# A three-block transformer on one core: the weight slots begin 64 bytes later in each partition

## The reference, cut to what matters

```python
x = layer_norm(x);  h = x @ w_in;  mix = mixer(h) @ w_out;  x = norm(alpha * x + mix)
ff = square(relu(x @ w1 + b1)) @ w2 + b2;                   x = norm(alpha * x + ff)
```

## Time and profile before

| | us |
|---|---|
| three runs | 3723.48, 3723.66, 3726.18 |
| median | 3723.66 |
| profiled execution, first to last instruction | 3724.2 |
| TensorE busy with matmuls | 3666.2 (98%) |
| VectorE busy | 2145.1 (58%) |
| ScalarE busy | 1580.6 (42%) |

### The profile page before, as it was taken

How to read it: one execution, slowest core, us unless ns; L and a number is a source line. 1 busy time by engine, 2 the same in 40 slices (tenths; PEclk the granted TensorE clock), 3 DMA queues, 4 the chain that set the end, 5 groups by cost and what they waited for, 6 DMA issues and landing times.

```text
span 3724.2 us, 50652 instructions
## 1 busy us (share of the span) xinstructions
PE 3666.2 (98%) x21121; PEld 2969.4 (80%) x21121; DVE 2145.1 (58%) x3262; ACT 1580.6 (42%) x2544; POOL 80.6 (2%) x85
## 2 busy tenths in 40 slices
PE   8999899999999999999999999999999999999998
PEld 5887778778888878888788889888787788788887
DVE  5641687775335578757587563366555266555333
ACT  5451566644334444435344452333343333434333
POOL 0000121000000000000000000000000000000000
PEclk9999899999999999999999999999999999999999
DMA  5124321324322222222222222222222222223232
GB/s 198 46 73 109 75 68 50 117 91 115 103 94 96 91 81 80 95 92 95 85 80 92 96 91 86 91 85 80 85 97 91 91 85 85 80 96 114 96 96 85
DMA packets 118490, 340.27 MB, mean 91 GB/s; under 512 B 20072, under 2 KB 31864, under 8 KB 118136
## 3 DMA queue, kind: packets, MB, share of 16 engines
q1 hardware_dynamic: 116024, 331.52, 27.3%
q0 software_dynamic: 2240, 5.51, 0.7%
HBM read 318.47 MB, written 20.06 MB: 91 GB/s over the span
## 4 chain that ended last, share of the span: by engine, by line
PE 95%; DVE 3%; ACT 1%; issue 1%; DMA 0%; SPq 0%; ACTq 0%; DVEq 0%
PE ps L329 54%; PE ps L307 28%; PE ps L1324 1%; PE ps L808 1%; PE ps L2833 1%; PE ps L1032 1%; PE ps L1647 1%; PE ps L1680 1%; PE ps L1335 1%; DVE n_s L1769 1%; PE ps L2262 0%; DVE g_D L1511 0%; PE ps L2289 0%; PE ps L1367 0%; PE ps L2251 0%
## 5 line engine op out<-in xcount | busy, mean ns | idle before, releaser
L329 PE MATMUL ps<-a,w_hi 128*128 128x512 f32 (+1 forms) x6064 | 1838.2, 388 | 2.5 <-ACT l_vf L2669 0.8
L329 PEld LDWEIGHTS ps<-a,w_hi 128*128 128x128 f32 x6064 | 1110.0, 188 | 259.5 <-issue 10.6
L329 PE MATMUL ps<-a,w_lo 128*128 128x512 f32 (+1 forms) x3032 | 1147.2, 385 | 0.0
L268 DVE TENSOR_TENSOR w_lo<-w_raw,w_hi 128x1024 fp32r<-128x1024 f32 x539 | 658.0, 1221 | 400.1 <-ACT w_hi L263 397.3
L263 ACT ACTIVATE w_hi<-w_raw 128x1024 fp32r<-128x1024 f32 x539 | 563.4, 1050 | 513.1 <-DMA w_raw<-in_w_mlp 324.1
L329 PEld LDWEIGHTS ps<-a,w_lo 128*128 128x128 f32 x3032 | 562.5, 188 | 120.0
L307 PE MATMUL ps<-h_hi,w_hi 128*128 128x512 f32 x1528 | 485.5, 399 | 0.0
L307 PE MATMUL ps<-h_lo,w_hi 128*128 128x512 f32 x1528 | 478.9, 395 | 0.0
L307 PE MATMUL ps<-h_hi,w_lo 128*128 128x512 f32 x1528 | 478.9, 395 | 0.0
L374 DVE TENSOR_TENSOR h_lo<-u_sq,h_hi 128x512 fp32r<-128x512 f32 x192 | 132.9, 692 | 460.7 <-ACT h_hi L364 459.8
L390 DVE TENSOR_TENSOR xT<-xT,ps 128x1024 f32<-128x1024 f32 x191 | 232.9, 1219 | 247.0 <-PE ps L307 246.0
(11 more groups left out here) (392 smaller groups left out, 2957.0 us busy)
## 6 DMA issues: line engine op xcount, KB each, us to landing
w_raw<-in_w_mlp SPq DMA_DIRECT2D x384, 512.0 KB, 3.4
w_raw<-in_w_in SPq DMA_DIRECT2D x107, 512.0 KB, 3.4
w_raw<-in_w_out SPq DMA_DIRECT2D x48, 512.0 KB, 3.4
n_bias<-na_tab SPq DMA_DIRECT2D x36, 256.0 KB, 4.7
xT<-in_x SPq DMA_DIRECT2D x8, 512.0 KB, 8.9
x<-xT SPq DMA_DIRECT2D x2, 2048.0 KB, 8.4
g_row<-gate_rows SPq DMA_DIRECT2D x16, 256.0 KB, 3.3
xT<-x SPq DMA_DIRECT2D x2, 2048.0 KB, 12.7
```

What stands on the lines that cost most here:

```text
L268: nc.vector.tensor_tensor(w_lo[u.z][:, :], w_raw[u.z][:, :], w_hi[u.z][:, :].bitcast(F32), ALU.subtract).then_inc(w_split[u.z], 1)
L329: last = nc.tensor.matmul(ps[:, bank, 0:t1 - t0], w[:, k * P:(k + 1) * P], a[:, h, low, k, t0:t1], start=(i_k == 0 and i == 0), stop=(i_k ...
```

## The change

A gap of 64 bytes is put ahead of the slots and one of 192 bytes behind them. So the slots move by 64 bytes, and everything behind them by 256. `slots_at` follows the slots.

```diff
         x_at = keep.at
         xT = keep.take("xT", [P, DC, T])
+        keep.at += 64
+        w_at = keep.at
         w_raw, w_lo, w_hi = [], [], []
         for z in range(SLOTS):
             w_lo.append(Region(keep.at, end).take(f"w_lo{z}", [P, UNIT], F32R))
             w_raw.append(keep.take(f"w_raw{z}", [P, UNIT]))
             w_hi.append(keep.take(f"w_hi{z}", [P, UNIT], F32R))
+        keep.at += 192
         params = keep.take("params", [P, NPARAM])
...
-        slots_at = [x_at + 4 * DC * T + 8 * UNIT * z for z in range(SLOTS)]
+        slots_at = [w_at + 8 * UNIT * z for z in range(SLOTS)]
```

## The result

The changed kernel takes 3703.7 us (four runs, 3702.55 to 3705.16) against 3723.57 us before (four runs): the ratio is 0.9946, with a 95% interval from 0.9934 to 0.9958. That is 20 us, or 0.54%, less; the forecast was 3716, and the range began at 3707. The profiled execution has a span of 3701.5 us, 22.7 less than before.

The account below looks back on a forecast made before the run. TensorE was taken to bound the kernel: the number of dense matmuls times the distance between their starts. 3724.2 less 8.2 us from down products, all else counted 0, gave 3716.0, given as 3716; range 3707 to 3735.

Parts of the forecast that it names:

- Step 1: MLP down products, 4584 matmuls: distance goes from 64 to 0, mean pace from 231.8 to 230 ns, 8.2 us less.
- my ends: Bounds for the down products' pace at distance 0: 229.1 ns low, 231.1 high; 12.3 or 3.1 us less.
- Steps 2, 3 and 4: Projections and up products 0, 2 us allowed either way; loads and splits 0; mixer tiles below 0.2 us, counted 0.
- The slots' place doesn't matter: Rival for the dense matmuls: lengths depend on the moving side alone, or distance 0 has two paces; 3724, chance 0.20.
- Distance 0 holds a longer step: Rival for down products: slower pace of 235.5 ns, 3741, or all at the slow pace, 3731; chance 0.22 together.

Follow-up runs that it names:

- e1_rings_only: Only the rings h_hi and h_lo begin 192 bytes later, against the kernel before, putting down products at distance 0: 3705.72 us against 3725.14, ratio 0.9948.
- e2_all_move: Every tile moved by 64 bytes, all distances kept, against the kernel before: 3726.96 us.
- e_compact: Activation rows of 2048 bytes for 2112, except block 3's first-half projection, against the changed kernel; such products at distance 0: 3665.45 us.
- m_64: No gap ahead of or behind the slots, against e_compact, so every dense product there is at distance 64: 3691.72 us.
- e_two_fast: w_hi of every slot at distance 0 and w_lo at 128, by gaps within the slots, against e_compact: 3722.24 us.
- e_hi_only: Only w_hi moved, to distance 0 from the rings, with w_lo left at 64, against the kernel before: 3713.18 us.

## Why the prediction was wrong

**The bound and the mechanism were right.** The dense stream sets the time, its pace depends on the distance, and distance 0 is the good one. e1_rings_only and e2_all_move show that the distance counts, and e_compact beside the table's other runs that 0 is the best of the seven held. The rule of the Trainium skill's page "SBUF — State Buffer" (section "Who interferes with whom"), by which TensorE's two reads are independent, would have given 3724. The map disagrees by 87 us from end to end (3752.44 to 3665.45), with the same instructions and only addresses changed.

**Step 1 failed, in the size of distance 0.** It put the pace at 230 ns, with 229.1 as the low end; 226.8 was measured (in the profile after). 4584 x (231.8 - 226.8) = 22.9 us, where I had 8.2. The reason is in how the number was found: I took the length of three matmuls at distance 0 inside a projection unit (392 and 389) as what distance 0 gives. Held alone, distance 0 shows 389 in every pass (the profile after, e_compact); in the mixture of e_two_fast the same reading gives 392 for it. A member of a mixture doesn't show the pace of its distance, and neither of my ends was a bound.

**Half of the gain was hidden in the kernel before.** Step 1 took the slow pace of 233.3 as one of two paces of distance 64. m_64 gives 228.9 for this distance where every product has it, in the same stretches. In the kernel before, the pace goes with how a stretch was entered, by the starts of all down products in its trace. The 29 stretches of 48 and more that follow directly on the matmul ahead of them (233 or 234 ns from start to start) all go at 233.3 ns. The other 20, of 47 and more, all go at 228.9 to 229.1, the one at 2666.91 us among them. Ahead of them a mixer's product comes in between, and the second down product starts only 319 to 634 ns after the first. One of these entries (start us, us), in which the pair of down products spans 0.74 us where an undisturbed pair spans 0.63:

```profile
876.40 0.81 PE L2110 MATMUL ps<-s_t,s_rel 32*8 32x384 f32 x2
877.14 0.74 PE L307 MATMUL ps<-h_hi,w_hi 128*128 128x512 f32 x2
```

e2_all_move has the same 29 and 20. In m_64, where the matmuls ahead are mostly at distance 64 too, 27 of the 29 directly entered stretches go at 228.9 to 229.0. The other two go at 233.3, one behind a projection that does so itself, the other behind the projection with rows of 2112 bytes (start us, us, what):

```profile
2355.24 11.20 PE ps L314 x48
```

So at distance 64 a stretch keeps the step that it is entered with; that the entry is the cause is argued from these counts, since no run changed the entry alone. In numbers: from the mean of 231.8 to 228.9 is 13 us of the 22.9, and from 228.9 to 226.8 the other 10.

**Steps 2, 3 and 4 held.** The projections' stretches are 22.26 for 22.24, at most 8376 / 96 x 0.02 = 1.7 us, within the 2 us allowed. Their circle of four distances was only begun elsewhere. Waits for slots haven't appeared, and block 1's small tiles can't be seen in the difference.

**The rivals.** "The slots' place doesn't matter", at 3724, fell with the result; by e1 and e2 the place alone indeed doesn't, but the distance does. "Distance 0 holds a longer step" was wrong for distance 0 and right in kind: 32, 96, 160, 192 and 224 do hold one, up to 234.2 ns. A gap of 128 bytes in place of 64, with 128 behind, would have put the down products at 192; I had no row by which to tell that.

**What stays open.** Why 0 is fast, 64 nearly so when well entered, and the other five slow; that the moving read and the weight load meet in some way is an argument from the addresses, and no run shows where. Whether the partner is the load of the following tile or of its own was not told apart. The pace of distance 128 held alone is unknown, and so is whether the distance counts modulo 256: of distances 256 bytes apart only 64 was held in both forms (64 modulo 512 in m_64, 320 in the kernel before), and it has both paces, 228.9 and 233.3, in either. In e_hi_only the `w_hi` of two slots is in fact 256 bytes off distance 0, and the paces of all four slots are the same.

## What to carry to other kernels

When TensorE never waits and the time still seems long, divide a back-to-back stretch of the chain by its number of matmuls. Where it is above the best pace of the same instruction elsewhere, look at the offset between the moving and the stationary operand, make it the same for all matmuls of the stream (here rows of 2048 bytes for 2112), and then try that one offset in 32-byte steps: in this kernel this moved the time from 3665 to 3752 us. Work out from the finished layout which offset an edit gives: two of the gaps here left it where it was. Don't price a distance from single matmuls of a mixed stream.

## What the runs showed of the hardware that was not expected

An fp32r matmul of 512 columns with a new 128 x 128 weight tile each time has a pace of 226.7, 228.9, 233.3 or 234.2 ns, at one granted clock, by the distance of its operands. At distance 64 the same stream has two steady paces, 228.9 and 233.3 ns, and keeps for up to 96 matmuls the one that it is entered with (49 of 49 long down stretches of the kernel before are sorted by the entry). A mixture of the distances 0 and 64 costs more than its members, 230.5 ns where they alone would average 229.0 at most (e_hi_only).
